# Fetching u and v of an expert in one 8 KB gather and working on them in pairs, in a two-layer backbone with a PEER mixer

## The reference

```python
def peer_ffn(h, wq, keys, u_tab, v_tab):
    q = (h @ wq).reshape(B, S, PEER_HEADS, 2, half)
    s = jnp.einsum('bshcd,hckd->bshck', q, keys).astype(jnp.float32)
    s_top, i_top = lax.top_k(s, PEER_TOPK)
    ...
    best_s, best_i = lax.top_k(cand, PEER_TOPK)
    ...
    experts = e1 * PEER_N_KEYS + e2
    gates = jax.nn.softmax(best_s, axis=-1).astype(h.dtype)
    ...
        u = jnp.take(u_tab, eb, axis=0)
        act = jax.nn.gelu(jnp.einsum('td,tkd->tk', xb, u))
        return jnp.einsum('tk,tkd->td', gb * act, jnp.take(v_tab, eb, axis=0))
```

## Time and profile before

| | us |
|---|---|
| median of 3 runs (2484.33 to 2493.12) | 2493.12 |
| profiled execution, first to last instruction (span) | 2660.3 |
| of it TensorE busy | 1716.3 |
| of it VectorE busy | 1616.4 |
| of it ScalarE busy | 337.3 |
| of it GpSimd busy | 1491.3 |
| first gather issued at | 211.32 |
| last step of the six jobs begins at | 656.1, 1062.1, 1477.5, 1907.6, 2291.5, 2648.2 |

### The profile page before, as it was taken

How to read it: one execution, slowest core, us unless ns; L and a number is a source line. 1 busy time by engine, 2 the same in 40 slices (tenths; PEclk the granted TensorE clock), 3 DMA queues, 4 the chain that set the end, 5 groups by cost and what they waited for, 6 DMA issues and landing times.

```text
span 2660.3 us, 24559 instructions
## 1 busy us (share of the span) xinstructions
PE 1716.3 (65%) x8433; PEld 893.7 (34%) x8433; DVE 1616.4 (61%) x3949; ACT 337.3 (13%) x998; POOL 1491.3 (56%) x1583
## 2 busy tenths in 40 slices
PE   6886759676376666366577585867638667435556
PEld 4564514342143422222344342435214342000101
DVE  3266775676865673954467964547866566854441
ACT  1320013101120100002110101311112010000000
POOL 1105466655656465566455664555665666766664
PEclk8987877888578778687688797788757878777779
DMA  8969899999999999999899999889999999999997
GB/s 315 422 252 364 314 389 367 390 370 394 368 328 401 358 411 413 404 411 410 314 366 387 369 411 355 317 336 354 410 380 328 395 379 411 389 357 377 364 367 296
DMA packets 248333, 980.68 MB, mean 369 GB/s; under 512 B 28001, under 2 KB 29681, under 8 KB 232849
## 3 DMA queue, kind: packets, MB, share of 16 engines
q0 software_dynamic: 226944, 847.35, 82.1%
q1 hardware_dynamic: 19536, 130.80, 12.3%
q10 hardware_dynamic: 1728, 0.95, 0.1%
HBM read 976.47 MB, written 2.52 MB: 368 GB/s over the span
## 4 chain that ended last, share of the span: by engine, by line
PE 17%; issue 12%; POOL 9%; DMA 8%; another core or an unknown queue 8%; DVE 7%; ACT 1%; SPq 0%; DVEq 0%; ACTq 0%; POOLq 0%
POOL expert L660 9%; PE acc L968 6%; DMA expert<-in_experts,eidx_t 4%; DVE expert L1529 3%; PE mmb L911 2%; DMA expert<-in_experts,eidx 2%; PE mmb L779 2%; PE mmb L860 1%; PE ob L887 1%; DMA wt<-in_w_wq 1%; PE trb L867 1%; PE mmb L743 1%; ACT hT L1048 1%; DVE small L1216 0%
## 5 line engine op out<-in xcount | busy, mean ns | idle before, releaser
L660 POOL DMA_INDIRECT expert<-in_experts,eidx x768 | 736.1, 958 | 648.0 <-PE acc L968 261.2
L1529 DVE CUSTOM_DVE_ANT_0 expert<-expert,hb 128x1024 f32<-128x1024 f32 x768 | 904.3, 1218 | 268.1 <-DMA expert<-in_experts,eidx 211.2
L660 POOL DMA_INDIRECT expert<-in_experts,eidx_t x768 | 730.5, 951 | 329.7 <-issue 212.5
L968 PE MATMUL acc<-expert,strip 128*32 128x512 f32 x3072 | 710.8, 725 | 262.2 <-DMA expert<-in_experts,eidx_t 190.5
L968 PEld LDWEIGHTS acc<-expert,strip 128*32 128x32 f32 x3072 | 135.0, 123 | 737.5 <-DMA expert<-in_experts,eidx_t 399.5
L911 PE MATMUL mmb<-hT,wt 128*128 128x128 f32 x1472 | 211.8, 307 | 58.2 <-issue 31.4
L911 PEld LDWEIGHTS mmb<-hT,wt 128*128 128x128 f32 x1472 | 200.3, 220 | 86.7 <-issue 68.9
L769 PE MATMUL mmb<-wt,hT 128*128 128x244 f32 x736 | 178.6, 404 | 33.4 <-issue 12.9
L769 PEld LDWEIGHTS mmb<-wt,hT 128*128 128x128 f32 x736 | 152.8, 211 | 64.6 <-issue 35.3
L1399 DVE TENSOR_REDUCE neg_max<-mmb 128x1 f32<-128x384 f32 (+1 forms) x120 | 55.1, 466 | 165.1 <-PE mmb L860 83.5
L942 PE MATMUL trb<-ident,acts 128*128 128x128 f32 x24 | 9.6, 398 | 171.0 <-DVE acts L1549 100.9
(11 more groups left out here) (192 smaller groups left out, 1629.8 us busy)
## 6 DMA issues: line engine op xcount, KB each, us to landing
wt<-in_w_wq SPq DMA_DIRECT2D x46, 1152.0 KB
expert<-in_w_mod POOLq DMA_DIRECT2D x39, 1024.0 KB, 13.8
wt<-in_w_win SPq DMA_DIRECT2D x30, 976.0 KB
wt<-in_w_wout SPq DMA_DIRECT2D x24, 1024.0 KB
expert<-in_experts,eidx POOLq DMA_INDIRECT x768
expert<-in_experts,eidx_t POOLq DMA_INDIRECT x768
wt<-in_w_mod SPq DMA_DIRECT2D x8, 1024.0 KB
wt<-in_w_uq SPq DMA_DIRECT2D x6, 384.0 KB
```

The source lines that it names most:

```text
L660: pool.indirect_dma_start(expert[:, g % RING, :], None, table, bass.IndirectOffsetOnAxis(at, 0)).then_inc(landed[g % RING], 16)
L968: m = pe.matmul(acc[32 * i:32 * i + 32, cs], strip[:, q % 2, i, at:at + 32], expert[:, (g + i) % RING, cs], start=k < 4, stop=False, skip_ ...
L1529: v.tensor_tensor_reduce(expert[:, r, :], expert[:, r, :], hb[:], 1.0, 0.0, ALU.mult, ALU.add, dots[:, k:k + 1]).then_inc(dot_ready, 1)
```

## The change

The indices are now used on another layout. A job has four chunks of 32 tokens. For each chunk, a gather has 32 tokens by 4 slots on its 128 partitions and brings the whole 8 KB row of each expert, u and v together, into one of 8 ring rows of 8 KB per partition. So a job has 128 gathers of 1 MB in place of 256 of 512 KB. A run is the 32 gathers of one chunk; the first job takes chunks 0 and 1 in half runs first, since only half of its search is done then.

- `hb` holds the 32 tokens of a chunk four times over, one copy for each group of 32 partitions. It is filled anew for each run by 32 products of `hT` with the identity (step `h_b`), after the last dot of the run before.
- Gathers are worked on in pairs. Step `u`: VectorE does two dots and three operations on 128x2 elements; ScalarE does a tanh, two operations that make the weights, and two copies of the fixed selection matrix `sel`, scaled by the weight of each partition, into `strip`. Step `v` stands one pair behind: TensorE multiplies the v half of both rows with these strips, in four groups of columns with 256 features each.
- A ring row is free only when its v products are done.
- The pairs are spread evenly over the estimated costs of the side work. In the first job at most 16 pairs go ahead of the second half of the search.
- The transposes of `idx_t` and `act`, the steps `gelu` and `act`, and `e1_each` go. ScalarE spreads the indices and the gates onto the new layout with 32 small copies for each half of a search.
- The sums lie in `acc` in another order, so ScalarE copies them into `tmp` before the last step, 8 copies in step `out` for chunks 0 and 2 and 8 for chunks 1 and 3.
- The tiles of the modulation weights use the 8 ring rows, instead of seven pairs of rows and one place in `wide`.

```diff
-RING = 15
+RING = 8
 WRING = 3
 HALF = SLOTS // 2
-PART = SLOTS // 4
-TOKS = P // PART
-STRIP = PART * PART // TOKS
+TOKS = 32
+PER = P // TOKS
+RUN = SLOTS // PER
+PAIR = 2
+PAIRS = SLOTS // PAIR
+CHAIN = 16
 GELU_C = (2 / math.pi) ** 0.5
...
-        if n == WQ_T - 1:
+        if n == (R_HEADS // 2 + 1 if (l, b) == (0, 0) else WQ_T - 1):
             out += [("idx_t", l, s, b, 0)]
...
+BEHIND = 1
+OUT_BEHIND = 3
+HALF_RUN = RUN // 2
+EARLY_RUNS = ((0, 0, HALF_RUN), (1, 0, HALF_RUN), (0, HALF_RUN, RUN), (1, HALF_RUN, RUN), (2, 0, RUN), (3, 0, RUN))
+RUNS = [EARLY_RUNS] + [tuple((c, 0, RUN) for c in range(PER))] * (3 * L - 1)
+ORDER = [[(c, m) for c, m0, m1 in runs for m in range(m0, m1)] for runs in RUNS]
+H_RUNS = list(itertools.accumulate((len(runs) for runs in RUNS), initial=0))
+def block_pairs(l, b):
+    runs = {}
+    at = 0
+    for n, (c, m0, m1) in enumerate(RUNS[3 * l + b]):
+        runs[at] = n
+        at += m1 - m0
     out = []
...
+    for p in range(PAIRS + BEHIND):
+        k = PAIR * p
+        now = []
+        if p < PAIRS:
+            if k in runs:
+                now.append(("h_b", l, "", b, runs[k]))
+            now.append(("u", l, "", b, k))
+        if p >= BEHIND:
+            now.append(("v", l, "", b, k - PAIR * BEHIND))
+        if k == (PER - 1) * RUN + PAIR * OUT_BEHIND:
+            now.append(("out", l, "", b, 0))
+        out.append(now)
+    return out
...
+def weave(l, b, side):
+    pairs = block_pairs(l, b)
+    out, at = [], 0
+    cost, done = sum(cost_of(x) for x in side), 0
+    searched = ("idx_t", l, "P" if b == 0 else "S", b, 1)
+    def pairs_to(n):
+        nonlocal at
+        if searched in side and searched not in out:
+            n = min(n, RUN // PAIR)
+        while at < n:
+            out.extend(pairs[at])
+            at += 1
+    pairs_to(1)
     for x in side:
         out.append(x)
-        done += 0 if x in beside else cost_of(x)
-        gathers_to(4 + sum(w <= ahead[-1] * done / cost + 1e-6 for w in ahead[1:]))
-    gathers_to(2 * SLOTS)
+        done += cost_of(x)
+        pairs_to(1 + int((PAIRS - 1) * done / cost + 1e-6))
+    pairs_to(len(pairs))
     return out
...
+            for g in range(3 * L * SLOTS):
+                i, k = divmod(g, SLOTS)
+                chunk, m = ORDER[i][k]
+                if chunk == 0 and m % HALF_RUN == 0:
+                    pool.wait_ge(idx_placed, 2 * i + m // HALF_RUN + 1)
+                if g >= RING:
+                    pool.wait_ge(slot_done, g - RING + 1)
+                pool.indirect_dma_start(expert[:, g % RING, :], None, t_in["experts"],
+                                        bass.IndirectOffsetOnAxis(eidx_t[:, i % 2, RUN * chunk + m:RUN * chunk + m + 1], 0)
+                                        ).then_inc(landed[g % RING], 16)
...
                     for kt in range(KT):
-                        pe.transpose(hb[:, kt * P:(kt + 1) * P], hT[:, kt, b * P:(b + 1) * P], ident[:]).then_inc(h_placed, 1)
+                        for c in range(PER):
+                            m = pe.matmul(hb[TOKS * c:TOKS * (c + 1), kt * P:(kt + 1) * P],
+                                             hT[:, kt, b * P + TOKS * chunk:b * P + TOKS * (chunk + 1)], ident[:], start=True, stop=True)
+                    m.then_inc(h_placed, 1)
...
+                    i = 3 * l + b
+                    chunk, m0 = ORDER[i][e]
+                    if e == 0 and i == 0:
+                        pe.wait_ge(mods_summed, SUMS)
+                    if m0 == 0 and chunk < 2 and i > 0:
+                        pe.wait_ge(acc_read, 2 * (i - 1) + chunk + 1)
+                    pe.wait_ge(strip_ready, PAIRS * i + e // PAIR + 1)
+                    at = chunk % 2 * 512 + chunk // 2 * 256
+                    for k in range(e, e + PAIR):
+                        r = (SLOTS * i + k) % RING
+                        for c in range(PER):
+                            m = pe.matmul(acc[TOKS * c:TOKS * (c + 1), at:at + 256], strip[:, r, :],
+                                          expert[:, r, D + 256 * c:D + 256 * (c + 1)], start=m0 + k - e == 0, stop=False,
                                           skip_group_check=True)
-                            if half == 1:
-                                m.then_inc(slot_done, 1)
+                        m.then_inc(slot_done, 1)
...
+                    i, turn = 3 * l + b, HALF // PER
+                    if e == 0 and i >= 2:
+                        act.wait_ge(slot_done, SLOTS * (i - 1))
+                    def spread(dst, src):
+                        for chunk, c in itertools.product(range(PER), range(PER)):
+                            m = act.activation(dst[TOKS * c:TOKS * (c + 1), i % 2, RUN * chunk + turn * e:RUN * chunk + turn * (e + 1)],
+                                               src[TOKS * chunk:TOKS * (chunk + 1), HALF * e + turn * c:HALF * e + turn * (c + 1)],
+                                               ACT.Copy)
+                        return m
+                    act.wait_ge(idx_ready, 2 * i + e + 1)
+                    spread(eidx_t, e1).then_inc(idx_placed, 1)
+                    act.wait_ge(gates_ready, 2 * i + e + 1)
+                    spread(gate_t, gate).then_inc(gates_placed, 1)
+                if kind == "u":
+                    g = SLOTS * (3 * l + b) + e
+                    act.wait_ge(cubic_ready, g // PAIR + 1)
+                    cs = slice(g % CHAIN, g % CHAIN + PAIR)
+                    link(act.activation(tanh[:, cs], cubic[:, cs], ACT.Tanh, scale=GELU_A * GELU_C))
+                    for q in range(PAIR):
+                        c = slice(g % CHAIN + q, g % CHAIN + q + 1)
+                        m = act.activation(weight[:, c], tanh[:, c], ACT.Identity, bias=gated[:, c], scale=gated[:, c])
+                    link(m)
+                    for q in range(PAIR):
+                        c = slice(g % CHAIN + q, g % CHAIN + q + 1)
+                        m = act.activation(strip[:, (g + q) % RING, :], sel[:], ACT.Copy, scale=weight[:, c])
+                    m.then_inc(strip_ready, 1)
+                if kind == "out":
+                    done = SLOTS * (3 * l + b + 1) - (RUN if e == 0 else 0)
+                    act.wait_ge(slot_done, done)
+                    for chunk, c in itertools.product((e, e + 2), range(PER)):
+                        at = e * 512 + chunk // 2 * 256
+                        m = act.activation(tmp[TOKS * chunk:TOKS * (chunk + 1), 256 * c:256 * (c + 1)],
+                                           acc[TOKS * c:TOKS * (c + 1), at:at + 256], ACT.Copy)
+                    m.then_inc(acc_read, 1)
...
+                    run = [n for n, (c, a, _) in enumerate(RUNS[i]) if (c, a) == (chunk, m0)]
+                    if run:
+                        v.wait_ge(h_placed, H_RUNS[i] + run[0] + 1)
+                    if chunk == 0 and m0 % HALF_RUN == 0:
+                        v.wait_ge(gates_placed, 2 * i + m0 // HALF_RUN + 1)
+                    g0 = SLOTS * i + e
+                    for g in range(g0, g0 + PAIR):
+                        r, c = g % RING, g % CHAIN
                         v.wait_ge(landed[r], 16 * (g // RING + 1))
-                        v.tensor_tensor_reduce(expert[:, r, :], expert[:, r, :], hb[:], 1.0, 0.0,
-                                               ALU.mult, ALU.add, dots[:, k:k + 1]).then_inc(dot_ready, 1)
+                        v.tensor_tensor_reduce(expert[:, r, 0:D], expert[:, r, 0:D], hb[:], 1.0, 0.0,
+                                               ALU.mult, ALU.add, dots[:, c:c + 1]).then_inc(dot_ready, 1)
+                    cs = slice(g0 % CHAIN, g0 % CHAIN + PAIR)
+                    v.wait_ge(dot_ready, g0 + PAIR)
+                    v.tensor_tensor(square[:, cs], dots[:, cs], dots[:, cs], ALU.mult)
+                    link(v.tensor_tensor(gated[:, cs], dots[:, cs], gate_t[:, i % 2, RUN * chunk + m0:RUN * chunk + m0 + PAIR], ALU.mult))
+                    v.scalar_tensor_tensor(out=cubic[:, cs], in0=square[:, cs], scalar=1.0 / GELU_A, in1=dots[:, cs],
+                                           op0=ALU.add, op1=ALU.mult).then_inc(cubic_ready, 1)
...
```

271 lines of the change are left out of this document (55 added, 216 removed).

## The result

The changed kernel takes 2694.98 us (median of 4 runs, 2686.4 to 2699.91) against 2488.72 us of the kernel before on the same chip (4 runs, 2482.67 to 2493.12): a ratio of 1.0828, 95% interval 1.0796 to 1.0861. It is 206 us slower; the forecast was 2440 us and faster, with 2580 us as the upper end.

The account below looks back on a forecast made before the run. The prediction took transfers as the bound, though not all the time: 2660.3 - 40 - 43 - 25 + 20 + 15 + 13 + 4 = 2604 us profiled, x 0.937 = 2440 us; range 2330 to 2580 us.

Parts of the forecast that it names:

- What bounds the kernel now: Six gather stages: bound by transfers, but not all the time; better feeding could win at most 210 us.
- factor of 0.937: Whole kernel: median run 2493.12 us over the profiled span, used to scale the 2604 us sum to 2440 us.
- The transfers, -40: Gathers with the queue full: 8 KB rows run at 420 instead of 409 GB/s; -40 us, bounds 0 and -58.
- GpSimd's issue, -43: First five stages: half as many gathers to issue, so faster refilling after stops; -43 us, a quarter of 173.
- The last stage, -25: Last stage: u and v in pairs leave no phase where one engine frees rows; -25 us, bounds -37 and 0.
- VectorE, +20: Three added operations per pair, 230 us of work, mostly hidden under transfers; 9% visible, +20 us.
- ScalarE, +15: New work per pair, 1.5 us each, 576 us in all; 2 to 3% visible, +15 us, bounds 0 and 576.
- TensorE, 0 and +13: v products cost the same, 0; 26 copies of h, 83 us of work, cost +13 us, bounds 0 and 83.
- the sign of too small a term: Copies of h: VectorE standing over 3 us at each of the 26 runs would show +13 us too small.
- The handshake: Rival, 27%: rows freed only after VectorE, ScalarE and TensorE in turn; 85 uncovered pairs pay 2.1 us each, 2575 us.
- the 290 that were named: Attention: a DMA rate under 290 GB/s, with TensorE waiting for ScalarE's strip, would mean uncovered pairs.
- The shorter ring: Rival, 16%: only four of eight rows remain as cover, 10 us; 15 stops lose 4 us each, +60, 2496 us.

Follow-up runs that it names:

- old deal: The changed kernel, with input-projection steps again at no cost when pairs are dealt over side work, as the kernel before did: 2625.66 us, ratio 1.057.
- undisturbed execution: A second profiled execution of the kernel before, without edits: 2484.38 us, ratio 0.9999, profiled span 2490.3 us against 2660.3 us in the first.
- everything out: Changed kernel without ScalarE's pair work, TensorE's products not waiting for VectorE, h copied once per block, input projections at no cost in dealing pairs: 2492.5 us.
- Three orders of the hand-off: Changed kernel, projections uncosted in dealing: ScalarE a pair later with TensorE two behind (2668.24 us) or one behind (2748.43); products right behind their dots (2943.35).
- the run with its products free: Changed kernel without ScalarE's pair work, TensorE's products waiting only for landed rows, rows freed after both dot and product: 2578.41 us, ratio 1.0406.

## Why the prediction was wrong

The account of the 206 us. Each line is a difference of two kernels, in the medians and in the sums of their six stages:

| | us | in the stages | forecast |
|---|---|---|---|
| deal of pairs (2694.98 - 2625.66) | 69 | 57 | not seen |
| ScalarE behind VectorE (2625.66 - 2546.53) | 79 | 77 | +15 for all of ScalarE |
| copies of h (2625.66 - 2598.28) | 27 | 28 | +13 |
| TensorE behind VectorE (2603.84 - 2578.41) | 25 | 31 | not seen |
| sum | 201 | 194 | |
| all four at once (2694.98 - 2492.5) | 202 | 195 | |

The second and third line are taken with the old deal, the fourth without it. Taken from the changed kernel, ScalarE gives 89 to 91 us and h 37, and the four make 222, 20 more than all at once. So they are separate but for some 20 us, which count twice where the deal is bad. In the stages 9 us are left over the kernel before, from 55 us won by the rate and 64 us of further gaps.

*What bounds the kernel now: the step that failed first.* The 210 us that "all that better feeding can win" came to were 30 us in an undisturbed execution. The factor of 0.937, read as "the profiled execution is slower throughout", should have stopped me: a profile 6.7% above every run is not a uniformly stretched one. With 30 us to win, -43 and -25 could not both be had. The forecast took 108 us off for three gains and put 52 on for all costs; what the costs came to was 202 us in the four lines above and some 64 in gaps beside them.

*The transfers, -40.* Right in its mechanism: 420.8 against 410.4 GB/s in full stretches, with side work too, worth 55 us at the bytes of the stages (the bounds were 0 and -58). The time doesn't show it, because more gaps take it back: even with the four costs and the small operations gone the kernel is at 0.998 of before.

The Trainium skill (DMA: Bandwidth & Descriptors, Anatomy of one DMA) fits one transfer as 2.0 us plus its bytes at 436 GB/s. Read so that only the bytes count once the queue is full, as in the prediction, it makes the two sizes equal there. The traces differ by 3%, 421 against 409 GB/s in the last stages, and the measurement decides.

*GpSimd's issue, -43.* 768 gathers of 0.954 us, busy 755.7 instead of 1487.7 us, as forecast. No gain shows: gaps in the transfers grew from 37 to 296 us, and 1544.3 of the 1716.0 us that GpSimd waits in them end with TensorE freeing a row, in which its own pace has no part. Its stops of over 6 us are 95 instead of 12, but also 72 with everything out, so their number alone says little. (0.524 MB in 1.24 us are 423 GB/s, not 421; nothing hangs on it.)

*The last stage, -25.* Measured -25.9, but that is luck: 9.7 MB less lay in it, and these are 24 us at its rate.

*VectorE, +20.* 183 us busy instead of 230, and 13 us visible where the other costs were gone. In the changed kernel, where the three operations stand ahead of ScalarE and TensorE, their cost was not measured.

*ScalarE, +15: mis-sized.* The work was right (rows of 202, 379 and 313 ns, busy 933.8 us for a forecast of 960). But it was priced as work, with "2 to 3% visible", and not as a wait: the sentence "it now waits in program order behind the dots of every pair, so the copies that free TensorE's banks queue behind VectorE" named a mechanism and put no price on it. Measured 79 to 91 us for following VectorE, and no difference between leaving the instructions out and doing them ahead (2603.84 against 2605.94). How much of it is ScalarE's standing and how much the 1.5 us that every row is held longer stays open.

*TensorE, 0 and +13.* The products take 1.07 us for 16 records at full clock and 1.94 at half, as in the earlier trace rows. Their wait behind the pair, 25 us, was not counted. The copies of h are busy 72.6 us for a forecast of 83, VectorE stands 128.1 us for them in 21 waits, 6.1 us each, where over 3 us was named as the sign of too small a term, and they cost 27, twice the term.

*Not in the sum.* The edit in `weave` that counts input projections as cost stood in the diff and was costed nowhere; it is the second largest cost, 69 us (57 in the stages).

*The rivals.* The handshake (27%) was the right one in kind: 283 GB/s in attention, under the 290 that were named, and TensorE waiting for the strip. Its price per uncovered pair, 2.1 us, was the work of the chain alone, and 85 pairs were to pay it, 179 us. The two hand-offs measured 79 and 25 us, less than that; its 2575 us were passed because the gains that it kept did not show in the time and the deal of pairs came on top. The shorter ring was right as well, as what turns a late engine into lost transfers: the changed ring loses 5.5% where the old one loses 1.2%. My reading is that they aren't two cases but one mechanism; no run takes them apart.

What stays open: the standing of programs against the holding of rows; what the gaps behind the stages cost, for which no run was made; why the fourth stage keeps 18 us over before with everything out (402.5 against 384.4, for the same 156 MB), where the stop of 23.94 us shown above is one part and the granted clock, 0.77 against 0.89, could be another; and a form that keeps the one gather and frees u early. Three orders of the hand-off (2668, 2748 and 2943 us) were all slower than the one of the change with the old deal (2626 us), which is the best complete version of the new layout found, 5.7% behind the kernel before.

## What to carry to other kernels

When the transfers are already full, larger ones with the same bytes can win only what their rate wins, 3% here, while each hand-off that a buffer must pass before it is free costs time even where the engine has work for a third of the span only; price a new wait by how long it holds the buffer and by what is queued behind it, not by the instructions that it adds. When a kernel with its costs taken out comes to the old time, look whether it gets there in the old way: here a gain of 55 us and a loss of 64 lay under a difference of 9. When a profiled execution is several per cent above all runs, its gaps aren't the kernel's: compare it with the runs before reading losses from it. And when a list is re-dealt, read how the deal counts its costs: a change of one weight was worth 57 to 69 us here.

## What the runs showed of the hardware

- Gathers of 8 KB rows ran at 421 GB/s and of 4 KB rows at 409 to 410 GB/s with the queue full, both on random rows; the difference holds in stages with side work and in the last one.
- One gather of 128 indices takes GpSimd 0.95 us whatever the row's size (0.954 and 0.949 to 0.956 us).
- The mean granted clock is 0.84 of full speed before and 0.70 after. In the last stage it is 0.54 (before 0.80), where TensorE works in pieces of 1.94 us between waits. In the run with its products free it was 0.72 in the second and third stage, which took no longer for it.
- From 100 to 150 us, ahead of the first gather, the granted clock was 0.74 in some profiled executions (the changed kernel, the undisturbed one of before) and 0.98 in others (the old deal, everything out), though the changed kernel and the old deal have the same steps there; the first gather came at 219 to 221 us in the former and at 210 in the latter.
- 537 us of work on ScalarE made no difference when done ahead of the pairs (2605.94 us against 2603.84 without it); behind VectorE it cost 79 to 91.
